# Two decoder layers on one core: expert weights loaded by whole experts, rotary partners fetched by DMA, and half of the first projection in three products

## What is computed

```python
h = rms_norm(x, norm1)
z = h @ w_in                        # 1024 x 3072, split into za, bq, bk, bv, cq, ck, cv, cg
a_out = causal_spatial_gating(gelu(za), ...)
b_out = dilated_attention(bq, bk, bv)          # 8 heads x 64
ro = retention(rotary(cq), rotary(ck), cv)     # 4 heads x 64
c_out = silu(cg) * group_norm(ro) * ret_gn
x = x + concat(a_out, b_out, c_out) @ w_out

# rotary: x1, x2 are the halves of 32 of a head's 64 columns
concat(x1 * cos - x2 * sin, x1 * sin + x2 * cos)

# hierarchical MoE: 16 experts, each token goes to 2 of one group of 4
for e in range(16):
    he = silu(t @ w_gate[e]) * (t @ w_up[e])   # 1024 -> 512
    y = y + combine[:, e:e+1] * (he @ w_down[e])
x = x + y
```

## Time and profile before

| | |
|---|---|
| median of 3 runs | 702.59 us (701.43 to 703.89) |
| profiled execution | 701.2 us, its span 699.4 us |
| TensorE busy | 662.6 us (95%) |
| VectorE busy | 298.5 us (43%) |
| ScalarE busy | 192.0 us (27%) |
| moved by DMA | 240.96 MB, 345 GB/s over the span |
| granted TensorE clock | 0.996 of full speed |
| chain that ended last | 75% TensorE, 22% DMA |

### The profile page before, as it was taken

One profiled execution on the slowest core, in us unless ns is written; L12 is line 12 of the kernel. 1 busy time (PEld: TensorE's weight loads), 2 busy tenths in 40 slices (PEclk: granted clock), 3 DMA queues, 4 the chain that ended last, 5 costly groups with the idle time before them and its releaser, 6 DMA issues.

```text
span 699.4 us, 9145 instructions
## 1 busy us (share of the span) xinstructions
PE 662.6 (95%) x3442; PEld 380.2 (54%) x3442; DVE 298.5 (43%) x632; ACT 192.0 (27%) x342; POOL 16.2 (2%) x29
## 2 busy tenths in 40 slices
PE   6999999999999999997999999999999999999883
PEld 5878778653444444431388878784543353352331
DVE  4478986611232122121474888673221322121234
ACT  3457543421111110100154554342201111111102
POOL 3100000200000000000020000000000000000000
PEclk9999999999999999999999999999999999999998
DMA  9985049999999999999986330998999999999991
GB/s 339 327 291 186 1 189 423 379 412 408 423 420 420 423 420 421 422 421 421 402 291 235 126 121 31 396 422 330 424 419 422 422 420 421 420 422 420 422 408 63
DMA packets 46027, 240.96 MB, mean 345 GB/s; under 512 B 3457, under 2 KB 3649, under 8 KB 21281
## 3 DMA queue, kind: packets, MB, share of 16 engines
q1 hardware_dynamic: 44800, 238.21, 84.2%
q0 software_dynamic: 1040, 2.04, 1.2%
q10 hardware_dynamic: 144, 0.13, 0.1%
HBM read 239.32 MB, written 1.05 MB: 344 GB/s over the span
## 4 chain that ended last, share of the span: by engine, by line
PE 75%; DMA 22%; DVE 1%; issue 1%; ACT 1%; DVEq 0%; SPq 0%
PE psum L1086 23%; PE psum L765 22%; DMA up_w<-in_w_up 21%; PE psum L1119 10%; PE psum L785 4%; PE psum L1066 3%; PE psum L1027 2%; PE psum L745 1%; PE psum L991 1%; PE psum L932 1%; DMA x<-in_x 1%; PE psum L1100 1%; PE psum L844 1%; PE psum L801 1%; PE psum L820 0%
## 5 line engine op out<-in xcount | busy, mean ns | idle before, releaser
L1086 PE MATMUL psum<-up_w,xT 128*64 128x512 f32 x512 | 114.2, 594 | 9.8 <-DMA up_w<-in_w_up 9.8
L1119 PE MATMUL psum<-down_w,scores 128*64 128x512 f32 x512 | 113.5, 595 | 0.0
L765 PE MATMUL psum<-piece_hi,hT_part 128*128 128x512 f32 x320 | 100.1, 394 | 0.0
L1086 PEld LDWEIGHTS psum<-up_w,xT 128*64 128x64 f32 x512 | 36.9, 137 | 83.7 <-issue 64.5
L1119 PEld LDWEIGHTS psum<-down_w,scores 128*64 128x64 f32 x512 | 36.6, 137 | 63.9 <-issue 61.6
L765 PEld LDWEIGHTS psum<-piece_hi,hT_part 128*128 128x128 f32 x320 | 59.0, 188 | 13.2 <-issue 1.7
L1523 DVE TENSOR_TENSOR y_lo<-psum,y_hi 128x512 fp32r<-128x512 f32 x32 | 22.1, 691 | 101.9 <-ACT y_hi L701 101.9
L765 PE MATMUL psum<-piece_lo,hT_part 128*128 128x512 f32 x160 | 62.4, 390 | 0.0
L1086 PE MATMUL psum<-gate_a,xT 128*64 128x512 f32 x256 | 56.9, 594 | 5.0 <-DMA gate_a<-in_w_gate 5.0
L1086 PE MATMUL psum<-gate_b,xT 128*64 128x512 f32 x256 | 56.4, 593 | 0.0
L1502 DVE SCALAR_TENSOR_TENSOR work<-work,psum 128x512 f32<-128x512 f32 x16 | 11.0, 687 | 105.2 <-ACT work L690 105.2
(11 more groups left out here) (243 smaller groups left out, 834.0 us busy)
## 6 DMA issues: line engine op xcount, KB each, us to landing
up_w<-in_w_up SPq DMA_DIRECT2D x32, 2048.0 KB, 17.2
down_w<-in_w_down SPq DMA_DIRECT2D x64, 1024.0 KB, 14.4
gate_b<-in_w_gate SPq DMA_DIRECT2D x32, 1024.0 KB, 14.4
gate_a<-in_w_gate SPq DMA_DIRECT2D x32, 1024.0 KB, 18.3
up_w<-in_w_in SPq DMA_DIRECT2D x6, 2048.0 KB, 13.2
down_w<-in_w_in SPq DMA_DIRECT2D x4, 2048.0 KB, 20.7
down_w<-in_w_out SPq DMA_DIRECT2D x4, 2048.0 KB, 8.1
up_w<-in_w_in SPq DMA_DIRECT2D x4, 1024.0 KB, 8.8
```

What stands on the lines that cost most here:

```text
L765: ins = pe.matmul(o, tokens, w[b][:, c, :], start=(c == 0 and n == 0), stop=(c == DC - 1 and n == len(parts) - 1))
L1086: ins = pe.matmul(psum[e * SLOTS:(e + 1) * SLOTS, bank, :], xT[:, c, k:k + SLOTS], w[:, e, c, :], start=(c == 0), stop=(c == DC - 1))
L1119: ins = pe.matmul(psum[e * SLOTS:(e + 1) * SLOTS, 2 + n, :], heT[:, c, e * SLOTS:(e + 1) * SLOTS], down_w[:, e, c, n * COLS:(n + 1) * COLS ...
```

## The change

- **Whole experts.** A load of gate, up or down weights now brings one expert of the pair, in rows of 16 KB per partition. The semaphores count by expert. TensorE runs all chunks of expert 0, then all of expert 1, and `gated`, `upped`, `downed` count up after each expert. In the gate product of item 0 the first four chunks still alternate.
- **Partners by DMA.** The permutation matrix and its two products go. SP copies 32-partition blocks of qkc to the places of their partners in work1 with four DMAs; it waits for the gelu's end (work1 is free) and for qkc, and these waits stand ahead of the load of the second half of w_out. The sign is in the sine table.
- **Half of BQ.** Chunks 4 to 7 of BQ are rounded (ScalarE) and split (VectorE), and their products are three fp32r ones. In layer 0 the rounding comes after that of the tokens, in layer 1 before the copies of the transposed tokens. The sums of squares and the inverse roots of norm1 now stand behind the splits of BK.
- **Second scores.** `score(1)` is asked for in the middle of CVG's second token tile, not ahead of it.

```diff
-("sin", SEQ), ("swap", P),
+("sin", SEQ),
...
+    put("sin", np.sin(ang.astype(np.float64)) * np.where(i % HD < half, -1, 1)[:, None])
...
+                def load_experts(dst, src, loaded, used, g, q, back=0, experts=(0, 1)):
+                    for e in experts:
                         if used is not None:
+                            sp.wait_ge(used.sem, used.at(g, e + 1 - back * used.turn))
                             settle(sp)
+                        sp.dma_start(dst[:, e], src[bass.ds(q, 1), :, e].rearrange("q p c n -> (q p) c n")).then_inc(loaded[e].sem, 16)
...
                 for n in range(2):
+                    if n == 1:
+                        sp.wait_ge(gelu_done.sem, gelu_done.at(l, 1))
+                        sp.wait_ge(proj_copied_a.sem, proj_copied_a.at(l, CQK))
+                        for k in range(4):
+                            there, here = slice((k ^ 1) * HD // 2, ((k ^ 1) + 1) * HD // 2), slice(k * HD // 2, (k + 1) * HD // 2)
+                            sp.dma_start(work1[there], qkc[here].rearrange("p c t -> p (c t)")).then_inc(swapped.sem, 16)
                     load_piece(6 + n, ...)
...
+                act.activation(hT_parts[0][:], hT_first, ACT.Copy).then_inc(hT_hi_ready.sem, 1)
+                if l == 0:
+                    act.wait_ge(bq_loaded[1].sem, bq_loaded[1].at(l, 16))
+                    act.activation(piece_hi[0][last_half], piece[BQ][last_half], ACT.Copy).then_inc(bq_hi_ready.sem, 1)
+                split_hi(BK)
...
                 square(0, work0)
...
+                            if c == DC // 2:
+                                pe.wait_ge(hT_split.sem, hT_split.at(l, 1))
+                                pe.wait_ge(bq_split.sem, bq_split.at(l, 1))
                             for m in range(4):
+                                o, cols = psum[:, bank + m, 0:SEQ], slice(m * P, (m + 1) * P)
+                                if c < DC // 2:
+                                    pe.matmul(o, w[:, c, cols], hT_first[:, c, :], start=(c == 0), stop=False)
+                                    continue
+                                hi, lo = piece_hi[0][:, c, cols], piece_lo[BQ][:, c, cols]
+                                pe.matmul(o, hi, hT_parts[0][:, c, :], start=False, stop=False)
+                                pe.matmul(o, hi, hT_parts[1][:, c, :], start=False, stop=False)
+                                ins = pe.matmul(o, lo, hT_parts[0][:, c, :], start=False, stop=(c == DC - 1))
...
-                    for n in range(2):
-                        ins = pe.matmul(psum[:, 2 + n, :], C("swap"), qkc[:, 2 * n:2 * n + 2, :].rearrange("p c t -> p (c t)"),
-                                        start=True, stop=True)
-                    ins.then_inc(swapped.sem, 1)
-                    score(1)
-                project(CVG, swap_score)
+                project(CVG, spatial, lambda: score(1))
...
+                        for e in range(2):
+                            if begun == 0:
+                                pe.wait_ge(loaded[e].sem, loaded[e].at(turn_of, 16))
+                            for c in range(begun, DC):
+                                if bank == 0 and i % 2 == 0 and e == 0:
+                                    tokens_ready(pe, g0, i // GROUP, i % GROUP // 2, c)
+                                ins = hidden(e, c)
+                            ins.then_inc(done.sem, 1)
...
+                    for e in range(2):
+                        pe.wait_ge(down_loaded[e].sem, down_loaded[e].at(g0 + i, 16))
                         for n in range(2):
+                            if e == 0:
                                 pe.wait_ge(y_lo_ready.sem, y_lo_ready.item(g0, i, n - 1))
+                            for c in range(HC):
+                                ins = pe.matmul(psum[e * SLOTS:(e + 1) * SLOTS, 2 + n, :], heT[:, c, e * SLOTS:(e + 1) * SLOTS],
+                                                down_w[:, e, c, n * COLS:(n + 1) * COLS], start=(c == 0), stop=(c == HC - 1))
...
+                dve.wait_ge(bq_hi_ready.sem, bq_hi_ready.at(l, 1))
+                V.tensor_tensor(piece_lo[BQ][last_half], piece[BQ][last_half], piece_hi[0][last_half].bitcast(F32), ALU.subtract).then_inc(bq_split.sem, 1)
+                split_lo(BK, 0)
+                split_lo(BK, 1)
                 square()
...
+                dve.wait_ge(swapped.sem, swapped.at(l, 4 * 16))
+                V.tensor_tensor(partner, partner,
                                 C("sin").unsqueeze(1).to_broadcast([P, 4, SEQ]), ALU.mult).then_inc(swap_read.sem, 1)
```

More of the change, by code:

```diff
@@ L54 @@
 GELU_CUBE = 0.044715
-CONST_PARTS = [("ident", P), ("ones", P), ("logc", 3 * P), ("decay", 4 * 2 * P), ("cos", SEQ), ("sin", SEQ), ("swap", P),
+CONST_PARTS = [("ident", P), ("ones", P), ("logc", 3 * P), ("decay", 4 * 2 * P), ("cos", SEQ), ("sin", SEQ),
                ("before", P), ("slot", SLOTS), ("index", EXPERTS), ("causal", P)]
@@ L597, in _ @@
                 square(0, work0)
[L598 to L601, removed]
                 act.wait_ge(projected.sem, projected.at(l, BQ + 1))
@@ L767, in three_products, with project @@
                     return ins
-                def project(j, between=None):
+                def project(j, between=None, within=None):
                     w, bank = piece[j], PIECE_BANK[j]
@@ L792, in project @@
                                 between()
-                            ins = three_products(j, psum[:, bank + t, :], t, wait=(t == 0))
+                            ins = three_products(j, psum[:, bank + t, :], t, wait=(t == 0), between=within if t == 1 else None)
                         ins.then_inc(projected.sem, 1)
@@ L1078, in item, with hidden @@
                     for bank, w, loaded, turn_of, done in ((0, gate_w[o], gate_loaded[o], halves, gated), (1, up_w, up_loaded, g0 + i, upped)):
-                        for c in range(DC):
-                            if bank == 0 and i % 2 == 0:
-                                tokens_ready(pe, g0, i // GROUP, i % GROUP // 2, c)
-                            if c % 4 == 0:
-                                pe.wait_ge(loaded[c // 4].sem, loaded[c // 4].at(turn_of, loaded[0].turn))
-                            for e in range(2):
-                                k = (i % GROUP) * P + e * SLOTS
-                                ins = pe.matmul(psum[e * SLOTS:(e + 1) * SLOTS, bank, :], xT[:, c, k:k + SLOTS],
-                                                w[:, e, c, :], start=(c == 0), stop=(c == DC - 1))
-                            if c % 4 == 3:
-                                ins.then_inc(done.sem, 1)
+                        def hidden(e, c):
+                            k = (i % GROUP) * P + e * SLOTS
+                            return pe.matmul(psum[e * SLOTS:(e + 1) * SLOTS, bank, :], xT[:, c, k:k + SLOTS],
+                                             w[:, e, c, :], start=(c == 0), stop=(c == DC - 1))
+                        begun = 0
+                        if bank == 0 and i == 0:
+                            begun = DC // 2
+                            for e in range(2):
+                                pe.wait_ge(loaded[e].sem, loaded[e].at(turn_of, 16))
+                            for c in range(begun):
+                                tokens_ready(pe, g0, 0, 0, c)
+                                for e in range(2):
+                                    hidden(e, c)
+                        for e in range(2):
+                            if begun == 0:
+                                pe.wait_ge(loaded[e].sem, loaded[e].at(turn_of, 16))
+                            for c in range(begun, DC):
[3 more added lines that the diff above has]
+                            ins.then_inc(done.sem, 1)
                         if bank == 0 and i == 0:
```

77 lines of the change are left out of this document (29 added, 48 removed).

## The result

The changed kernel takes **877.05 us** (876.74 to 877.10, 4 runs) against 702.72 of the kernel before, run beside it: ratio 1.248, 95% interval 1.246 to 1.250. The forecast was 707.5. The sign was right, the size wrong by 170 us. The profiled execution took 877.1 us, its span 875.3.

The account below looks back on a forecast made before the run. It took TensorE to bound the kernel up to about 251 us, then the expert weight stream at 420 GB/s. Layer 0 +3.4 and layer 1 +2.2 gave 706.8 profiled, 708.2 against the median; it predicted 707.5, range 698.5 to 716.

Parts of the forecast that it names:

- the order of the expert matmuls: Expert products: running all of expert 0's matmuls before expert 1's leaves the two array halves overlapping; cost 0.
- Rival A: Expert stages: the array halves no longer overlap, each stage 13.9 us instead of 7.1, about 990 us; chance 0.10.
- Release: Expert buffers come free 3.5 us later, at stage end, delaying the weight queue: +3.0 us in layer 0, +3.4 in layer 1.
- Tail: End of each layer: expert 1 lands last and its 16 records run alone in one half, +3.4 us per layer.
- Larger rows: Expert weight stream: 16 KB rows instead of 8 KB save 1.5% of load time, -3.0 us per layer.
- BQ: Mixing stage: three products for half of BQ give -0.3 us in layer 0, limited by piece ZA, and -1.5 in layer 1.
- Partners and second scores: Mixing stage: TensorE arrives 1.8 us early and waits for VectorE, -0.1 us per layer; later scores 0, up to +0.2.
- The sum: Whole kernel: layer 0 +3.4 us, layer 1 +2.2, together +5.6; 706.8 in a profile, 708.2 against the median.

Follow-up runs that it names:

- late start: Kernel before, with each expert stage waiting for both halves of its weights before its first matmul: 708.87 us, ratio 1.0091.
- late release: Kernel before, with both counts that free an expert weight buffer moved to the end of the stage: 707.91 us, ratio 1.0084.

## Why the prediction was wrong

- **The step that failed: the order of the expert matmuls.** "So the later half was not held back by four records of the earlier one. I take it that 16 are no obstacle either: cost 0." The first sentence was right, and it was the whole truth: TensorE reached over exactly four records where one expert had eight or sixteen of them in a row. Rows 5 had runs of just that length, and the second sentence carried them four times as far. It cost 158 us (change with and without it) or 184 (alone). The rows bounded it from one side only: they showed 4 free, and nothing showed 16.
- **The size.** Rival A named the mechanism and gave 990 us, and "half of that", 846, for a queue that sees two matmuls ahead. Two fp32 matmuls are four records, and half the slots come back: a stage takes 24 slots between 16 and 32. Per item it is 36.27 - 24.0 = 12.3 us: 3 x 8 x 0.43 = 10.3 inside the stages, and 4 more slots, 1.7, for the unpaired ends where the queue has drained between up and down. Eight items make 98 us, of which TensorE's old waits for weights (9.8 + 5.0 in both layers, 7 in one) swallow a part: +91 per layer by this count. The first product of layer 1 starts at 439.4 us instead of 351.9: +87.5, with the mixing stage's gain of 1.3 in it, so +89. The 846 left out the drained ends (8 x 1.7 per layer, 27 of the 31 us between it and 877). The rule cited for A (the Trainium skill, TensorE: Matmul & The Clock Gate, Part 3: matmuls start and end in program order) is not what the traces show: expert 1's records start ahead of expert 0's later ones. But it pointed at the danger, and its direction was right. A had 0.10; with rows that bear out four records and none that bears out more, it should have had about half.
- **Release.** +6.4 forecast, +5.3 measured alone: right in size and place (mostly idle near 141 and 484).
- **Tail.** +6.8 forecast for an expert that lands last and runs alone. It can't be read apart from A in the changed kernel: its last down product takes 12.23 us. The nearest measurement is the late start, +6.3, which has a slower clock in it too.
- **Larger rows.** 1.5% forecast, 1.7% measured. In the changed kernel they can be worth little, since TensorE and not the stream is the bound there.
- **BQ.** -1.8 forecast, -3.3 measured by the medians, -2.2 between the profiles. "Only about 0.3 us of slack is there" took ZA's landing as fixed, and in layer 0 it came 2.8 us sooner; that the loads moved by the same change are the reason is possible, but not shown. The other term was too large: layer 1 gave 0.9, not 1.5. The two errors had opposite signs, so the -1.8 is nearer to the -2.2 than its terms were to theirs.
- **Partners and second scores.** -0.2 forecast, -0.4 (-1.1 to +0.3) measured: no change that can be told from none, which fits the reading that VectorE takes TensorE's saving.
- **The sum.** With the experts alternating, the forecast's parts would have given 707; 718.8 came. This gap belongs to that variant: alternating makes a stage wait for both experts, which the change doesn't do, and a late start and a late release together cost 7.5 more than one by one. By the single runs it is +19.1 for the two ends, -1.6 for the rows and -2.7 for the rest, 717 us. Whether whole experts would have given the forecast if the order were free can't be tried, since beyond four records it isn't.

## What to carry to other kernels

Here two column halves of TensorE overlapped only as far as it reached ahead, four records (two fp32 matmuls, four bfloat16 ones): alternate the halves at least every two fp32 matmuls, and don't give one half a long run because its data happen to come as a block. A coarser load costs at both ends of its buffer's ring, the start and the release (5.3 and 6.3 us here), and the two feed each other where engine and stream are close (19.1); 1.7% more bandwidth didn't pay for it. When a row supports a free order over some distance, price what lies beyond that distance from the other side.

## What the runs showed of the hardware that I had not expected

- The reach of four records, and that it is a count of records and not of matmuls or of time (1.7 us in fp32, 0.9 us in bfloat16). Within it the two halves run out of program order; behind it even an idle half waits.
- After a wait of 3.4 us the granted clock was 0.50 in a stretch of 5 us (0.92 and 0.91 in the stretches beside it), with the work already back; that stage took 9.84 us instead of 7.1. With late start alone, waits of 2.86 and 2.89 us were followed by stages of 8.6 and 8.8 us, one of 1.15 by a stage of 7.1. The kernel before waits for weights only half a stage at a time, up to 1.4 us, and keeps 0.996; with late start and late release the mean is 0.982.
- Loads of 2 MB in rows of 16 KB per partition: 428 GB/s, against 421 for loads of 1 and 2 MB in rows of 8 KB.
- Where small parameter loads of POOL were issued at 26 us and not at 16, a 2 MB piece that had been on its way beside them was there some 2 us sooner (28.8 to 30.7 us, against 30.8 to 32.6). The squares and splits moved with them, so the cause is not isolated.
